# Dense products of a hybrid decoder step: per row tile, first the products with the rounded weights, then those with the remainder

## What is computed

```
z = rms_norm(x) @ w_in                       # 2048 x 5120: q | k | v | conv pair
x = x + concat(attention(q, k, v), conv(u)) @ w_out      # 2048 x 2048
h = rms_norm(x) @ w_up                       # 2048 x 8192
y = x + square(relu(h)) @ w_down             # 8192 x 2048
```

## Time and profile before

| | |
|---|---|
| median of 3 runs | 1945.98 us (1945.96 to 1946.32) |
| profiled execution | span 1942.3 us from first to last instruction; its own time is not listed apart, the runs lie 3.7 us above the span |
| TensorE matmul busy | 1855.0 us, 96% of the span |
| VectorE busy | 941.6 us, 48% |
| ScalarE busy | 712.3 us, 37% |
| mean granted TensorE clock | 0.983 |

### The profile page before, as it was taken

One profiled execution on the slowest core, in us unless ns is written; L12 is line 12 of the kernel. 1 busy time (PEld: TensorE's weight loads), 2 busy tenths in 40 slices (PEclk: granted clock), 3 DMA queues, 4 the chain that ended last, 5 costly groups with the idle time before them and its releaser, 6 DMA issues.

```text
span 1942.3 us, 37404 instructions
## 1 busy us (share of the span) xinstructions
PE 1855.0 (96%) x13315; PEld 1657.8 (85%) x13315; DVE 941.6 (48%) x1412; ACT 712.3 (37%) x1116; POOL 76.8 (4%) x132
## 2 busy tenths in 40 slices
PE   6998999999999889899979999999999999999999
PEld 4998987777777566676649999999999999999998
DVE  4567332323234588684624555444544444445544
ACT  4333222222222435454324444333433344334433
POOL 3000000000000290000000000000000000000000
PEclk9999999999999989899999999999999999999999
DMA  6445466666666545455654455445544555455543
GB/s 171 141 138 180 156 212 225 214 226 204 224 210 227 171 147 170 129 162 184 201 185 155 151 160 163 167 168 163 163 166 168 162 163 166 167 162 164 167 166 135
DMA packets 140971, 337.71 MB, mean 174 GB/s; under 512 B 11339, under 2 KB 11395, under 8 KB 140592
## 3 DMA queue, kind: packets, MB, share of 16 engines
q1 hardware_dynamic: 138688, 332.05, 52.8%
q0 software_dynamic: 2208, 4.74, 0.8%
HBM read 331.64 MB, written 5.96 MB: 174 GB/s over the span
## 4 chain that ended last, share of the span: by engine, by line
PE 88%; DVE 5%; issue 3%; ACT 2%; DMA 1%; DVEq 0%; POOL 0%; ACTq 0%; SPq 0%; POOLq 0%
PE acc L523 21%; PE acc L525 20%; PE acc L524 20%; PE aux L611 12%; PE aux L599 6%; PE aux L651 5%; PE acc L721 1%; DMA page<-in_cache_v 1%; PE acc L743 1%; DVE tmp L1523 1%; DVE w_lo L1211 1%; DVE z L1321 1%; ACT s_rows L982 0%; DVE tmp L1412 0%; PE aux L577 0%
## 5 line engine op out<-in xcount | busy, mean ns | idle before, releaser
L1211 DVE TENSOR_TENSOR w_lo<-raw,w_hi 128x1024 fp32r<-128x1024 f32 x368 | 450.8, 1225 | 533.2 <-ACT w_hi L885 530.4
L885 ACT CAST w_hi<-raw 128x1024 fp32r<-128x1024 f32 x368 | 386.3, 1050 | 649.7 <-PE acc L525 649.7
L523 PE MATMUL acc<-a_hi,w_hi 128*128 128x288 f32 (+1 forms) x1920 | 583.1, 304 | 10.0 <-DVE z L1218 4.0
L525 PE MATMUL acc<-a_hi,w_lo 128*128 128x288 f32 (+1 forms) x1920 | 572.9, 298 | 0.0
L524 PE MATMUL acc<-a_lo,w_hi 128*128 128x288 f32 (+1 forms) x1920 | 572.1, 298 | 0.0
L523 PEld LDWEIGHTS acc<-a_hi,w_hi 128*128 128x128 f32 x1920 | 362.8, 189 | 25.8 <-issue 17.1
L524 PEld LDWEIGHTS acc<-a_lo,w_hi 128*128 128x128 f32 x1920 | 362.8, 189 | 0.5
L525 PEld LDWEIGHTS acc<-a_hi,w_lo 128*128 128x128 f32 x1920 | 363.1, 189 | 0.0
L525 PE MATMUL acc<-h_hi,w_lo 128*128 128x288 f32 x1024 | 302.2, 295 | 0.0
L524 PE MATMUL acc<-h_lo,w_hi 128*128 128x288 f32 x1024 | 301.5, 294 | 0.0
L523 PE MATMUL acc<-h_hi,w_hi 128*128 128x288 f32 x1024 | 301.3, 294 | 0.0
(11 more groups left out here) (202 smaller groups left out, 1004.5 us busy)
## 6 DMA issues: line engine op xcount, KB each, us to landing
page<-in_cache_k SPq DMA_DIRECT2D x128, 512.0 KB, 4.7
page<-in_cache_v SPq DMA_DIRECT2D x128, 512.0 KB, 4.3
raw<-in_w_up SPq DMA_DIRECT2D x128, 512.0 KB, 3.7
raw<-in_w_down SPq DMA_DIRECT2D x128, 512.0 KB, 3.6
raw<-in_w_in SPq DMA_DIRECT2D x80, 512.0 KB, 3.8
raw<-in_w_out SPq DMA_DIRECT2D x32, 512.0 KB, 3.7
out<-y_nat SPq DMA_DIRECT2D x8, 256.0 KB, 2.6
x_nat<-in_x_prompt SPq DMA_DIRECT2D x1, 1024.0 KB, 9.3
```

The costliest lines, as they stand in the source:

```text
L523: mm(out, wh, ah, start=(kt == 0), stop=False)
L525: last = mm(out, wl, ah, start=False, stop=(kt == KT - 1))
L885: nc.scalar.copy(w_hi[:, j % SPL], raw[:, j % RAW]).then_inc(hi_ok, 1)
L1211: v.tensor_tensor(w_lo[:, j % SPL], raw[:, j % RAW], w_hi[:, j % SPL].bitcast(F32), ALU.subtract)\
```

## The change

In `products` the loop over m is split. In row tiles 0 to 14 TensorE now issues for all four m the two products with `w_hi`, and after them for all four m the product with `w_lo`. At the first row tile of a chunk it waits for `hi_ok` ahead of the first part and for `lo_ok` ahead of the second. In the first row tile of a visit the wait for `acc_free` of bank m stands ahead of `rounded(m)`. Row tile 15 keeps the order of before, m by m, and signals `acc_ok` as before; `w_used` is signalled by the last matmul of a chunk as before. The number of matmuls, weight loads and bytes stays the same.

```diff
+                def rounded(m):
+                    mm(acc[:, m, 0:width], weights(w_hi, m), ah, start=(kt == 0), stop=False)
+                    mm(acc[:, m, 0:width], weights(w_hi, m), al, start=False, stop=False)
+
+                def rest(m):
+                    return mm(acc[:, m, 0:width], weights(w_lo, m), ah, start=False, stop=(kt == KT - 1))
+
                 if kt % CK == 0:
-                    pe.wait_ge(lo_ok, RAW + NC * n + kt // CK + 1)
-                for m in range(MT):
-                    if kt == 0:
-                        pe.wait_ge(acc_free, MT * n + m + 1)
...
-                    mm(out, wh, ah, start=(kt == 0), stop=False)
-                    mm(out, wh, al, start=False, stop=False)
-                    last = mm(out, wl, ah, start=False, stop=(kt == KT - 1))
-                    if kt == KT - 1:
-                        last.then_inc(acc_ok, 1)
-                    elif kt % CK == CK - 1 and m == MT - 1:
+                    pe.wait_ge(hi_ok, NC * n + kt // CK + 1)
+                if kt < KT - 1:
+                    for m in range(MT):
+                        if kt == 0:
+                            pe.wait_ge(acc_free, MT * n + m + 1)
+                        rounded(m)
+                    if kt % CK == 0:
+                        pe.wait_ge(lo_ok, RAW + NC * n + kt // CK + 1)
+                    for m in range(MT):
+                        last = rest(m)
+                    if kt % CK == CK - 1:
                         last.then_inc(w_used, 1)
+                else:
+                    for m in range(MT):
+                        rounded(m)
+                        rest(m).then_inc(acc_ok, 1)
```

More of the change, by code:

```diff
@@ L512, in products, with weights @@
                 slot = kt // CK % SPL
-                if kt % CK == 0:
-                    pe.wait_ge(lo_ok, RAW + NC * n + kt // CK + 1)
-                for m in range(MT):
-                    if kt == 0:
-                        pe.wait_ge(acc_free, MT * n + m + 1)
[L518 to L522, removed]
-                    mm(out, wh, ah, start=(kt == 0), stop=False)
-                    mm(out, wh, al, start=False, stop=False)
-                    last = mm(out, wl, ah, start=False, stop=(kt == KT - 1))
-                    if kt == KT - 1:
-                        last.then_inc(acc_ok, 1)
-                    elif kt % CK == CK - 1 and m == MT - 1:
+                t = kt if tile is None else tile
+                ah, al = hi[:, t, c0:c0 + width], lo[:, t, c0:c0 + width]
+                def weights(w, m):
+                    return w[:, slot, kt % CK, P * m:P * (m + 1)]
+                def rounded(m):
[3 more added lines that the diff above has]
+                    return mm(acc[:, m, 0:width], weights(w_lo, m), ah, start=False, stop=(kt == KT - 1))
+                if kt % CK == 0:
+                    pe.wait_ge(hi_ok, NC * n + kt // CK + 1)
[9 more added lines that the diff above has]
+                    if kt % CK == CK - 1:
                         last.then_inc(w_used, 1)
+                else:
+                    for m in range(MT):
+                        rounded(m)
+                        rest(m).then_inc(acc_ok, 1)
             pe.wait_ge(consts, CONSTS)
```

## The result

The changed kernel's first four runs have a median of 1956.92 us (1956.26 to 1962.72), beside 1945.97 us for the kernel before (1941.73 to 1946.32, four runs): a ratio of 1.0069 with a 95% interval of 1.005 to 1.0088, about 11 to 13 us slower where 6.1 were forecast. Two later sets of the same kernel (experiments 5 and 9), with more runs of both, gave 1.0035 (1.0013 to 1.0057) and 1.0045 (1.0024 to 1.0065). All 26 runs of the changed kernel together have a median of 1952.5 us and a mean of 1954.7; 104 runs of the kernel before have 1947.0 and 1946.7. (One execution of 3598 us is left out.)

What follows compares the result with a forecast made beforehand. TensorE, busy in 96% of the span, was taken as the bound. A loss of 10.1 us less gains of 4.0 gave +6.1 on the 1942.3 us span; with 3.7 for runs, 1952.1 us, range 1948.0 to 1957.5.

Steps and rivals of the forecast that it cites:

- Bank 3 wanted before VectorE's fourth take: First row tile of a visit: bank 3 wanted after six matmuls, not nine; 0.25 us per ordinary start, loss 10.1 us.
- the third place: What is left of the 3.7 us of waits for the remainder; eight rounded products cover it, gain 0.4 us.
- The stall that the earlier trace gave: At visit starts, a product waiting for its bank counts from 0.16 us after VectorE's take.
- The gain at the three waits: Waits for w_lo in visit 0, the first w_out visit and a third place: 4.0 us, 2.6 if the clock falls anyway.
- The fall of the clock in visit 0: Behind chunk 2's wait the clock fell to 0.50 for 3.41 us; counted as gone, gain 1.4 us.
- The pace in the stream: Eight bank changes per row tile instead of four in the matmul stream; claimed to cost 0.
- The rival in which the changes of bank make the clock fall: Bank rotation or new waits drop the clock in each of 46 visits: 69 us, 2021 us; chance 0.03.
- the step "Sum": Whole kernel: +10.1 - 4.0 = +6.1 us on the 1942.3 us span, plus 3.7 us for runs, giving 1952.1 us.
- the 3.7 us between the span of before and its runs: Whole kernel before: its runs lie 3.7 us above its profiled span; added to the forecast span of 1948.4 us.
- Rival C: Attention stage: the new order itself lowers the granted clock there; set up for the experiments, no chance given.

Runs made afterwards that it cites:

- experiment 1: Changed kernel, but row tile 0 of every visit keeps the old order; median 1946.0 us, ratio 0.9987 to the kernel before.
- experiments 2, 3 and 6: 2: split order only in row tile 0, 1960.6 us; 3: kernel before plus 12 transposes, 1946.9; 6: changed kernel with the old wait for the remainder, 1955.1.
- experiment 7: Changed kernel, but row tile 0 finishes banks 0 and 1 before banks 2 and 3; median 1942.3 us, ratio 0.9984 to the kernel before.
- experiment 8: Changed kernel with row tile 0 in the old order, plus six filler transposes ahead of each step of the last attention body; median 1946.4 us.

## Why the prediction was right and where it failed

**Direction and mechanism were right.** Bank 3 wanted before VectorE's fourth take is the loss: split in row tile 0 alone it costs 10.4 us at equal clock (forecast 10.1), and without the split there nothing of it stays (experiment 1). In the profiles the steps come out one by one: from visit 12 to visit 45 (the third of w_out and the last of w_down, counted from 0) the changed kernel took 854.2 us and the old one 846.1. The forecast for those 33 starts, less the 0.4 us gained at the third place, which lies in visit 14, was 25 x 0.25 + 8 x 0.29 - 0.4 = 8.2; it is 8.1. The stall that the earlier trace rows gave (0.16 us behind the take) carried over to all of them. The working overlooked that banks 1 and 2 are wanted too early as well; as bank 3 is the last, its wait sets the sum.

Outside the attention stage, and so with no fit, the profile of before took 1568.4 us and the three of the changed kernel 1574.3, 1574.2 and 1575.3: +5.8 to +6.9, where 6.1 was forecast.

**The gain at the three waits was right within 0.5 us.** 4.0 was forecast; -3.6 us at equal clock in experiment 1. In the pair of profiles, place by place: 2.7 us in visit 0 (2.5 forecast), 1.1 in the first w_out visit (1.1) and 0.4 in visit 14 (0.4). The fall of the clock in visit 0 was rightly counted as gone: the four profiles with the wait at the front (before, experiments 2, 3 and 6) have it, the ten others don't. (The prediction works the fall out at 1.5 us and enters 1.4, and reads the end of the transposes as 42.2 where the row gives 42.30; neither matters.) The fall shows in the mean clock too, so the equal-clock figure may understate this part by up to 1 us.

**The pace in the stream** was right: 0 forecast, and 820 us in visits of w_up and w_down ran at a clock of 1.00. Behind the first row tile of a visit the matmuls there stand 0.1325 us apart on average, before and after. The rival in which the changes of bank make the clock fall does not show here.

**What failed is the step "Sum": that all else, the attention stage first, takes what it took before, and that a measurement tells 3.9 us.** The attention stage stood in the sum at 0, and no row had been read for how far its time varies; it gave 6.2 of the 12.1 us between the two profiles. I took the close three runs of before (within 0.4 us) for the scatter of this kernel. 104 runs of it go from 1941.6 to 1953.7 us, and 26 of the changed one from 1948.1 to 1969.2. The first four of the changed kernel have a mean 11.5 us above that of the 104 runs. By the fit 6.7 of them are there at equal clock, and 4.9 are their mean clock of 0.9752 against 0.9792; half of that is peculiar to those four, as all 26 runs have 0.9772.

That the stage's time goes with its clock, whichever the kernel, the profiles show. It took 373.9 us in the kernel before with the clock at 0.50 for 55 us, 377.7 with 66 in experiment 3 (the kernel before with transposes), and 373.7 with 61, 377.9 with 72 and 380.1 with 78 in the changed kernel. Part of this hid in the 3.7 us between the span of before and its runs. Every later run has a span 1.8 to 1.9 us below its own time, so about half of the 3.7 us was no constant: it was the difference between the profiled execution (clock 0.983) and three others.

The forecast of 1952.1 us is near the median of all 26 runs, 1952.5, and 4.8 us from the first set's. The first is in part luck: the median of before rose by 1.0 us with more runs, and the means lie 8.0 us apart.

**Open** is whether the change lowers the clock itself. Over all sets it is 0.9772 for the changed kernel (standard error 0.0008) and 0.9792 for the one before (0.0003): 0.0020, worth 2.5 us, and 8.0 us between the means against 5.3 to 6.7 at equal clock. The pairs of experiment 7, with the split in nearly every row tile, came at 0.9792. Twelve transposes near 190 us raised it by 0.0039 in the changed kernel (24 runs) and by 0.0046 in that of experiment 1, but not in the kernel before. That is more than the executions' scatter, and no run here shows why: neither the fall near 190 us nor the time of entering the stage accounts for it. Rival C is thus not shown and not excluded. Nor did an experiment raise the clock of the attention stage and so win time: the filler of experiment 8 raised it and lost. That the clock sets the stage's time rests on the runs and profiles above.

## What to carry to other kernels

When a loop's order changes, list every semaphore inside it by the time at which it is wanted, not only the one that the change is about: here a wait that almost never bound was moved later, and three that had about 0.1 us to spare (banks 1 to 3) were moved earlier. Put the new order only where it has something to hide: from row tile 1 on it wins 3.6 us at equal clock, everywhere it loses 5 to 7; paired by banks in row tile 0 it wins 2.7. Before forecasting a few us, look in the profile for stretches with a lowered granted clock; a kernel that has them scatters by more than three close runs suggest, and comparing runs at equal mean clock brought the scatter of a single run down to 1.2 us.

## What the runs showed of the hardware

A wait of 2.3 us in visit 0 was followed by 3.4 us at the half clock in all four profiles that had it. The waits of 1.1 to 1.3 us in the dense products of visit 0, of visits 2 to 4 and of the first w_out visit were followed by no fall. A stall of 0.25 us does not show as idle time at all, as TensorE's matmuls are drawn 0.29 us long at a distance of 0.13; it is read from start to start. The mean granted clock of one and the same kernel went from 0.967 to 0.981, and its time from 1969 to 1948 us with it.
